# Fills, weight splits and the squares of y moved between steps and engines in a state-space scan

## The reference, cut to what matters

```
y = ssd_chunked(x, dt, a, bm, cm)          # 32 heads of 64, 4 groups, one chunk of 256 tokens
y = y + d_skip * xs
y = y * silu(z)                            # 2048 channels
y = y.reshape(b, l, 4, 512)
y = y * rsqrt(mean(y * y, axis=-1) + 1e-6) # grouped norm: 4 groups of 512 channels
y = (y * norm_g) @ w_out                   # 2048 -> 1024
```

## Time and profile before

| | us |
|---|---|
| median of 3 runs | 965.77 |
| lowest, highest | 965.77, 967.42 |
| the profiled execution, device time | 968.91 |
| its span in the trace | 967.1 |
| PE busy | 929.4 |
| DVE, ACT, POOL busy | 563.3, 487.8, 36.1 |
| scan (from the wait behind its first step to the first matmul of w_out) | 143.5 to 213.43 |
| w_out | 213.43 to 262.0 |

### The profile page before, as it was taken

One profiled execution on the slowest core, in us unless ns is written; L12 is line 12 of the kernel. 1 busy time (PEld: TensorE's weight loads), 2 busy tenths in 40 slices (PEclk: granted clock), 3 DMA queues, 4 the chain that ended last, 5 costly groups with the idle time before them and its releaser, 6 DMA issues.

```text
span 967.1 us, 15638 instructions
## 1 busy us (share of the span) xinstructions
PE 929.4 (96%) x6624; PEld 860.2 (89%) x6624; DVE 563.3 (58%) x645; ACT 487.8 (50%) x670; POOL 36.1 (4%) x51
## 2 busy tenths in 40 slices
PE   7999999998999989999999999999999599999996
PEld 6999988787899889999988899987998499999885
DVE  6788465784565575455544854675755645554543
ACT  5566467764545564344433554665645534434332
POOL 1000001130000000000000220000000000000000
PEclk9999999999999999999999999999999799999999
DMA  8766442234653365555555697433643345555551
GB/s 261 260 187 192 145 153 89 88 127 138 204 188 128 127 209 187 173 174 186 189 190 189 218 266 220 132 131 131 217 138 115 119 143 191 188 174 174 197 194 44
DMA packets 121061, 163.80 MB, mean 169 GB/s; under 512 B 4076, under 2 KB 106916, under 8 KB 121012
## 3 DMA queue, kind: packets, MB, share of 16 engines
q1 hardware_dynamic: 117684, 151.99, 48.0%
q0 software_dynamic: 3328, 11.10, 3.7%
HBM read 162.01 MB, written 1.07 MB: 169 GB/s over the span
## 4 chain that ended last, share of the span: by engine, by line
PE 84%; DVE 10%; ACT 4%; issue 2%; DMA 1%; SPq 0%; DVEq 0%; ACTq 0%
PE bank L443 76%; DVE w_lo L1152 2%; DVE ntmp L1215 1%; PE bank L750 1%; PE bank L721 1%; DVE x L1218 1%; DVE ntmp L1194 1%; ACT ntmp L861 1%; PE bank L639 1%; PE bank L545 1%; DMA pre_row<-in_mix_pre_g_dram 1%; DVE stats L1183 1%; DVE stats L1185 1%; PE bank L805 1%; PE bank L677 0%
## 5 line engine op out<-in xcount | busy, mean ns | idle before, releaser
L1152 DVE TENSOR_TENSOR w_lo<-w_raw,w_hi 128x2048 fp32r<-128x2048 f32 x135 | 308.4, 2290 | 219.4 <-ACT w_hi L839 219.2
L443 PE MATMUL bank<-actT_hi,w_hi 128*128 128x256 f32 x1280 | 364.8, 285 | 4.8 <-DVE w_lo L1163 1.7
L443 PE MATMUL bank<-actT_lo,w_hi 128*128 128x256 f32 x1280 | 363.2, 284 | 0.0
L443 PE MATMUL bank<-actT_hi,w_lo 128*128 128x256 f32 x1280 | 363.1, 284 | 0.0
L839 ACT ACTIVATE w_hi<-w_raw 128x2048 fp32r<-128x2048 f32 x135 | 256.6, 1907 | 98.6 <-DMA w_raw<-in_ffn_w_down_dram 52.9
L443 PEld LDWEIGHTS bank<-actT_hi,w_hi 128*128 128x128 f32 x1280 | 246.7, 193 | 6.8 <-issue 4.6
L443 PEld LDWEIGHTS bank<-actT_lo,w_hi 128*128 128x128 f32 x1280 | 246.8, 193 | 0.1
L443 PEld LDWEIGHTS bank<-actT_hi,w_lo 128*128 128x128 f32 x1280 | 246.7, 193 | 0.0
L443 PE MATMUL bank<-w_hi,hT_hi 128*128 128x512 f32 x176 | 68.5, 389 | 0.0
L443 PE MATMUL bank<-w_lo,hT_hi 128*128 128x512 f32 x176 | 68.5, 389 | 0.0
L443 PE MATMUL bank<-w_hi,hT_lo 128*128 128x512 f32 x176 | 68.5, 389 | 0.0
(11 more groups left out here) (209 smaller groups left out, 1280.5 us busy)
## 6 DMA issues: line engine op xcount, KB each, us to landing
w_raw<-in_ffn_w_gu_dram SPq DMA_DIRECT2D x44, 1024.0 KB, 5.0
w_raw<-in_ffn_w_down_dram SPq DMA_DIRECT2D x22, 1024.0 KB, 4.9
w_raw<-in_ssm_w_in_dram SPq DMA_DIRECT2D x20, 1024.0 KB, 5.3
w_raw<-in_mem_w_kv_dram SPq DMA_DIRECT2D x16, 1024.0 KB, 5.6
w_raw<-in_ssm_w_out_dram SPq DMA_DIRECT2D x8, 1024.0 KB, 4.9
w_raw<-in_mem_w_q_dram SPq DMA_DIRECT2D x8, 1024.0 KB, 5.1
w_raw<-in_mem_w_o_dram SPq DMA_DIRECT2D x8, 1024.0 KB, 4.9
w_raw<-in_w_kv_dram SPq DMA_DIRECT2D x8, 1024.0 KB, 5.6
```

Source lines behind the costliest of these rows:

```text
L443: ins = pe.matmul(dst, a, b, start=first and n == 0, stop=last and n == len(passes) - 1, skip_group_check=True)
L1152: dve.tensor_tensor(lo[:, s, :], raw[:, s, :], hi[:, s, :].bitcast(F32), ALU.subtract).then_inc(w_lo_done, 1)
```

## The change

1. `SSD_FILLS`: the first ten of the twelve fills move one step earlier in the scan; the two of v0 1 stay in steps 16 and 17. The fill that stood in step 1 is now in step 0. `SSD_SPLITS` moves with it: from steps 1, 2, 4, 5, 7, 8, 10, 11, 13, 14, 16, 17 to 0, 1, 3, 4, 6, 7, 9, 10, 12, 13, 16, 17.
2. POOL squares y of each pair itself (16 multiplications of 128 x 256) before it adds (12 additions as before); ACT's 16 squares are gone. POOL now waits for `y_ready` of DVE, no longer for ACT.
3. ACT and DVE split w_out 2 and 3 (units 28 and 29) in step 19, ahead of the norm of the last group.
4. `ssd_ssq(3)` stands ahead of w_out 2 in PE's program, no longer ahead of w_out 1.

```
-SSD_FILLS = {1: ("k0", 0, 0), 3: ("k0", 0, 1), 4: ("k0", 1, 0), 6: ("k0", 1, 1), 7: ("k0", 2, 0), 9: ("k0", 2, 1),
-             10: ("k0", 3, 0), 12: ("k0", 3, 1), 13: ("v0", 0, 0), 15: ("v0", 0, 1), 16: ("v0", 1, 0), 17: ("v0", 1, 1)}
+SSD_FILLS = {0: ("k0", 0, 0), 2: ("k0", 0, 1), 3: ("k0", 1, 0), 5: ("k0", 1, 1), 6: ("k0", 2, 0), 8: ("k0", 2, 1),
+             9: ("k0", 3, 0), 11: ("k0", 3, 1), 12: ("v0", 0, 0), 14: ("v0", 0, 1), 16: ("v0", 1, 0), 17: ("v0", 1, 1)}
...
                 if n == 0:
                     for k in range(XT):
-                        if k % GT:
+                        total, y = ysum[:, k // GT % 2, :], z[:, k, :]
+                        pool.wait_ge(y_ready, k + 1)
+                        if k % GT == 0:
+                            if k >= 2 * GT:
+                                pool.wait_ge(ssq_mm, k // GT - 1)
+                            pool.tensor_tensor(total, y, y, ALU.mult).then_inc(ysq_ready, 1)
+                        else:
+                            if k > 2:
+                                pool.wait_ge(ysum_added, added(k - 1))
+                            pool.tensor_tensor(ysq[:, k % 2, :], y, y, ALU.mult).then_inc(ysq_ready, 1)
                             pool.wait_ge(ysq_ready, k + 1)
-                            if added(k) > 1:
-                                pool.wait_ge(ysum_added, added(k) - 1)
-                            total = ysum[:, k // GT % 2, :]
                             pool.tensor_tensor(total, total, ysq[:, k % 2, :], ALU.add).then_inc(ysum_added, 1)
...
-                if i == 1:
+                if i == 2:
                     ssd_ssq(SSM_GROUPS - 1)
                 pe.wait_ge(y_lo_done, i * MR // GT + 1)
...
-                if 1 <= c <= XT:
-                    k = c - 1
-                    act.wait_ge(y_ready, c)
...
-                    act.activation(square, z[:, k, :], ACT.Square).then_inc(ysq_ready, 1)
+                if c == XT + 1:
+                    hi_upto(U[("w_out", 3)])
                 if c > 1 and c % GT == 1:
...
+                if c == XT + 1:
+                    lo_upto(U[("w_out", 3)])
                 if c > 1 and c % GT == 1:
                     g = c // GT - 1
                     dve.wait_ge(rs_ready, g + 1)
```

## The result

The changed kernel takes 959.52 us (959.15 to 960.1, 4 runs) where the kernel before takes 965.8 us (965.77 to 967.42, 4 runs on the same chip): 6.3 us less, ratio 0.9935, 95% interval 0.9922 to 0.9947. In a later series on another chip, six and eleven runs, it was 960.73 against 967.09, ratio 0.9934 (0.9921 to 0.9948). The forecast was 957.8 with a range of 955 to 962.5; the time is inside it and 1.7 us above the forecast. The two profiled spans differ by more than the medians, 967.1 and 957.9 us. Of these 9.2 us, 1.2 lie ahead of the scan, 3.8 in the scan and 4.4 in w_out, less 0.2 behind them. Why single executions say more than the medians turned out to be the main lesson.

What follows compares the result with a forecast made beforehand. PE, busy 929.4 of 967.1 us, was taken as the bound, so only its idle and half-clock time could be gained. 2.3 + 1.4 + 0 + 4.3 = 8.0 us off the median 965.77 gave 957.8, range 955 to 962.5.

Steps and rivals of the forecast that it cites:

- The wait for `xtok`: Sign in the changed kernel's trace: waits for `xtok` under 1 us at step 2 and none at step 9.
- The term of 2.3 us: Start of the scan: a fill in step 0 uses PE's standstill; gain 2.3 us, 0.8 if a slow stretch comes anyway.
- the half clock is in this: 1.5 of the 2.3 us: Start of the scan: 1.5 us of the gain come from a fill that runs at full clock.
- a rival for the kernel after: Start of the scan: clock may still fall in the thin stretch 146.5 to 149.9; gain 6.5 us, 959.3; chance 0.17.
- place B: Scan step 9: PE waits for transposes and the second decay row; gain 1.4 us, bounds 0.7 and 1.4.
- Forecast 4.3 us: w_out: the 2.7 us pause before w_out 2 and 1.6 us of half clock behind it go; bounds 2.7 and 4.3.
- The 3 us to spare: w_out 4: its split is ready 7.9 us after the sum, with 10.9 us of w_out 2 and 3 as cover.
- the clock's part is safe: w_out: the slow stretch of 1.6 us has no reason to come without its pause.
- Booked at 0: Scan: squares on POOL cost PE nothing, as DVE's waits for PE absorb 2.9 us; upper bound of middle case 1.
- 0.18 us: Scan: DVE time lost per POOL instruction, from 2.2 us over 12; 16 more make DVE busy 2.9 us longer.
- mt multiplications with a mean under 1.15 us: Sign in the changed kernel's trace: DVE's mt multiplications stay under that mean, with 28 POOL instructions of 0.7 to 2 us.
- the last rival: Scan: POOL and DVE exclude each other in nearly every instruction; slower, 968.4; decides from 0.47 us per instruction; chance 0.05.

Runs made afterwards that it cites:

- The doubled squares: The changed kernel with POOL computing each square twice, 44 instructions in place of 28, same output; 962.29 us, 1.6 us more than the changed kernel.
- early_splits_only: Kernel before plus only the splits of units 28 and 29 ahead of the last norm; 964.42 us against 966.87, ratio 0.9974.
- ssq_only: Kernel before with only the later sum of squares, ahead of w_out 2, splits staying behind the norm; 973.49 us against 966.87, ratio 1.007.

## Why the prediction was right, and where its terms were off

**The start of the scan.** The pause that the fill took over stood behind a load of ACT's function table, which neither the prediction nor its rows name and which the change leaves in place; PE now has work beside it:

```profile
142.94 1.28 ACT L985 ACT_TABLE_LOAD   x1
```

The wait for `xtok` went, and the fill stands in its place, as forecast; step 3 was forecast 11.0 us behind step 0 and came at 10.7. The term of 2.3 us is the one that was mis-sized, and the step that failed is "the half clock is in this: 1.5 of the 2.3 us". Against the one profiled execution the term measured 2.67 us (10.48 + 2.87 - 10.68). But five of seven executions with the old start ran that fill at full clock, and against them it is 1.2 us. I had given the slow clock a rival for the kernel after, and none for its absence in the kernel before. Of the 1.7 us between forecast and median, 1.1 are here, 0.3 in place B and the others in the rest.

**Place B.** Forecast 1.4 us, measured 60.16 - 2.87 - 56.20 = 1.1 us; without POOL's squares 1.34. The mechanism was right, a new wait of 0.26 us took the rest.

**w_out.** Forecast 4.3 us, measured 4.4 in the trace and 4.3 in the medians, with the pause ahead of w_out 2 and its slow stretch both gone. The 3 us to spare were 2.9. That the clock's part is safe was too strong: one of six executions with the pause of 2.7 us did not have the slow stretch. The share of the two edits was not asked by the prediction. The later sum alone costs 6.6 us. The splits alone bring the whole gain in the length of the stage, 43.80 us as with both edits, but only 2.45 us in the median.

**POOL and DVE.** Booked at 0, measured at 0.26 us in the scan and nothing by itself. But the price for each instruction was twice the forecast: 0.39 and not 0.18 us. So the sign "mt multiplications with a mean under 1.15 us" did not come true, it was 1.17. The reason is in where the squares begin, just behind z, when DVE goes on with two-input instructions: seven of the nine slow mt multiplications began beside a square. The additions before came later, after ACT, and only two mt multiplications were slow. At 0.39 the last rival (which needed 0.47) was nearer than its 0.05 said, as far as its own rule goes. The doubled squares show that it would not have decided in that way, since POOL itself is late first. The Trainium skill, "SBUF — State Buffer", section "Who interferes with whom", has the exclusion that these rows agree with: 1172 ns in place of 956 on multiplications with two inputs from SBUF, and none on the `xbc` ones, which take one input from PSUM (472 and 476 ns).

**The rest.** From the last matmul of w_out to the end the profiled executions of all kernels have the same work and differ by up to 1.6 us, with 705.65 and 705.84 in the two profiles of the changed kernel against 705.1 to 705.4 in the four whose fills and w_out are as before. With 1.2 + 1.1 + 4.4 = 6.7 gained in the stages against a start that is warm, and 0.3 to 0.6 lost in the rest, the 6.3 us of the medians are reached. The loss is mostly PE's wait behind the load of `pre_row`, 0.26 and 0.55 us in these two profiles and none in those four. Whether the changed kernel brings that wait on is not shown: the three kernels that differ from it by one edit do not have it. The 1.9 us that early_splits_only misses in the median stay open.

## What to carry to other kernels

Before a stretch at half clock goes into a sum, look whether it belongs to the kernel or to the execution: two more profiles of the kernel before would have moved the forecast by a microsecond. Where one instruction stands behind a chain that crosses engines, look for independent work that can be issued ahead of the chain's wait; the four lines that split two weight units early took 4.4 us from w_out in the trace, where all the rest took 2.3 from the scan, though their median alone shows 2.45 us. And work moved to an idle engine that shares a port costs by when it begins, so the price must be taken from instructions that begin at the same point, not from those that happen to be there.

## What the runs showed of the hardware that was not expected

- The granted clock fell behind the same 2.7 us pause in five of six profiled executions and stayed at 1.00 in one, with the same instructions around it. At the start of the scan, behind waits of 1.35, 0.19 and 0.18 us, it fell in two of seven. Four of these seven had a fall at about 12 us after the start of the span, and none of the four had the one in the scan; of the three without it, two did. That one excludes the other is not shown by so few.
- Where it fell, it stood at 0.50 for 3.4 us (eight matmuls of 512 columns at 0.43 us and not 0.23), whether it began at once or 1.5 us behind the pause. In ssq_only it stood there for 10.2 us, 5.1 of them inside the pause of 8.0 us, and around the pause 505 us behind w_out it stood there for 13.7 us in all fourteen profiles.
- A square of 128 x 256 on POOL took 0.61 us where it began ahead of DVE's instruction and 1.53 us where DVE was already in one with two inputs from SBUF (at 188.24 and 193.73 in the changed kernel).
